# S5 recurrence of a streaming encoder step: one pass over all channel groups, or two passes over half of them

## The reference, cut to what matters

```python
a_bar = jnp.exp(lam * step)
b_bar = ((a_bar - 1.0) / lam)[:, :, None] * b_mat
bu = jnp.einsum('gph,blgh->blgp', b_bar, ug.astype(jnp.complex64))
bu = bu.at[:, 0].add(a_bar[None] * h0)
_, h = lax.associative_scan(_linear_recurrence, (a_seq, bu), axis=1)   # h[l] = a_bar*h[l-1] + bu[l]
y = jnp.einsum('gop,blgp->blgo', c_mat, h).real.reshape(bsz, l, D_SSM)
y = y + d.astype(f32) * uf
z = jax.nn.gelu(y)
out = z * jax.nn.sigmoid(z @ w_glu.astype(f32) + b_glu.astype(f32))
return out.astype(u.dtype), h_last.real, h_last.imag
```

## Time and profile before

| what | value |
|---|---|
| median of 3 runs | 2489.22 us (2488.09 to 2496.07) |
| profiled execution, its own time | 2488.07 us |
| its span | 2486.3 us |
| PE busy | 2303.2 us, 93% of the span |
| DVE, ACT, POOL busy | 44%, 40%, 47% of the span |
| mean granted TensorE clock | 0.969 of full |
| `ssm_run`, first matmul to first instruction of the next stage | 384.53 to 505.67 us |

### The profile page before, as it was taken

One profiled execution on the slowest core, in us unless ns is written; L12 is line 12 of the kernel. 1 busy time (PEld: TensorE's weight loads), 2 busy tenths in 40 slices (PEclk: granted clock), 3 DMA queues, 4 the chain that ended last, 5 costly groups with the idle time before them and its releaser, 6 DMA issues.

```text
span 2486.3 us, 32536 instructions
## 1 busy us (share of the span) xinstructions
PE 2303.2 (93%) x12461; PEld 2107.6 (85%) x12461; DVE 1088.6 (44%) x2093; ACT 1006.8 (40%) x1664; POOL 1167.8 (47%) x557
## 2 busy tenths in 40 slices
PE   6999926789868999999999999999999999999998
PEld 6999914445467999999999999999899999999998
DVE  3786774347654243444253343253343243432222
ACT  4555412147534343443344343344343343343432
POOL 3544575004334555554545454444454444455554
PEclk9999968899888999999999999999999999999999
DMA  5544410114115434355333354433354333344443
GB/s 142 145 132 128 103 41 5 1 50 96 61 51 150 129 116 119 115 152 149 119 101 113 104 164 122 119 102 106 98 156 125 115 102 110 107 132 136 131 127 103
DMA packets 542831, 272.13 MB, mean 109 GB/s; under 512 B 107292, under 2 KB 535893, under 8 KB 542165
## 3 DMA queue, kind: packets, MB, share of 16 engines
q1 hardware_dynamic: 542677, 270.06, 38.2%
HBM read 252.65 MB, written 17.43 MB: 109 GB/s over the span
## 4 chain that ended last, share of the span: by engine, by line
PE 69%; DVE 2%; issue 1%; DMA 0%; ACT 0%; POOL 0%; SPq 0%; DVEq 0%; ACTq 0%
PE ffn_bank L138 22%; PE ffn_bank L139 22%; PE ffn_bank L140 22%; PE ffn_bank L2356 1%; PE ffn_bank L2445 1%; PE ffn_bank L2327 1%; DVE ffn_nv L2060 0%; DVE ffn_mt L2070 0%; ACT ffn_w_hi L1807 0%; POOL ffn_w_lo L1797 0%; DMA ahead_w_raw<-in_w_down 0%; DMA ahead_w_raw<-in_w_gate 0%; DVE ffn_mt L2006 0%; DVE ffn_xm_lo L2107 0%; DVE ffn_xf_lo L2202 0%
## 5 line engine op out<-in xcount | busy, mean ns | idle before, releaser
L1797 POOL TENSOR_TENSOR ffn_w_lo<-ahead_w_raw,ffn_w_hi 128x1024 fp32r<-128x1024 f32 (+1 forms) x380 | 889.2, 2342 | 915.0 <-ACT ffn_w_hi L1807 914.8
L138 PE MATMUL ffn_bank<-ffn_xf_hi,ffn_w_hi 128*128 128x386 f32 (+5 forms) x1760 | 628.7, 357 | 15.4 <-DVE ffn_xf_lo L2202 11.4
L139 PE MATMUL ffn_bank<-ffn_xf_lo,ffn_w_hi 128*128 128x386 f32 (+5 forms) x1760 | 622.8, 354 | 0.0
L140 PE MATMUL ffn_bank<-ffn_xf_hi,ffn_w_lo 128*128 128x386 f32 (+5 forms) x1760 | 621.9, 353 | 0.0
L1807 ACT ACTIVATE ffn_w_hi<-ahead_w_raw 128x1024 fp32r<-128x1024 f32 (+1 forms) x380 | 391.7, 1033 | 505.9 <-PE ffn_bank L140 325.2
L138 PEld LDWEIGHTS ffn_bank<-ffn_xf_hi,ffn_w_hi 128*128 128x128 f32 x1760 | 332.4, 189 | 31.3 <-issue 16.8
L139 PEld LDWEIGHTS ffn_bank<-ffn_xf_lo,ffn_w_hi 128*128 128x128 f32 x1760 | 333.5, 189 | 12.9 <-issue 0.7
L140 PEld LDWEIGHTS ffn_bank<-ffn_xf_hi,ffn_w_lo 128*128 128x128 f32 x1760 | 333.0, 189 | 12.2
L138 PE MATMUL ffn_bank<-ffn_h_hi,ffn_w_hi 128*128 128x384 f32 (+2 forms) x880 | 312.4, 355 | 4.7 <-DVE ffn_xT L2150 3.6
L139 PE MATMUL ffn_bank<-ffn_h_lo,ffn_w_hi 128*128 128x384 f32 (+2 forms) x880 | 310.9, 353 | 0.0
L140 PE MATMUL ffn_bank<-ffn_h_hi,ffn_w_lo 128*128 128x384 f32 (+2 forms) x880 | 309.9, 352 | 0.0
(11 more groups left out here) (342 smaller groups left out, 3075.2 us busy)
## 6 DMA issues: line engine op xcount, KB each, us to landing
ahead_w_raw<-in_w_gate SPq DMA_DIRECT2D x220, 256.0 KB, 3.3
ahead_w_raw<-in_w_up SPq DMA_DIRECT2D x220, 256.0 KB, 3.2
ahead_w_raw<-in_w_down SPq DMA_DIRECT2D x160, 256.0 KB, 3.2
pin_w_raw<-in_w_in SPq DMA_DIRECT2D x120, 256.0 KB, 3.4
ahead_w_raw<-in_w_out SPq DMA_DIRECT2D x160, 128.0 KB, 2.7
ahead_w_raw<-in_w_down SPq DMA_DIRECT2D x80, 192.0 KB, 2.7
pin_xrow<-in_x_prompt SPq DMA_DIRECT2D x15, 512.0 KB, 6.1
out_y_prompt<-ffn_yrow SPq DMA_DIRECT2D x15, 512.0 KB, 4.8
```

Source lines behind the costliest of these rows:

```text
L138: pe.matmul(out, w_hi, x_hi, start=first, stop=False)
L139: pe.matmul(out, w_hi, x_lo, start=False, stop=False)
L140: return pe.matmul(out, w_lo, x_hi, start=False, stop=last)
L1797: pool.tensor_tensor(w_lo[n % 3][:, 0:c], w_raw[n % 2][:, 0:c], w_hi[n % 3][:, 0:c].bitcast(F32), ALU.subtract).then_inc(s_lo, 1)
```

## The change

The table's correction, the rotations, the scans and the edges run twice, each time over four of the eight pairs (`ps`), the first half first. `s_e` and `s_fin` count to 2, DVE starts a half when that half's table and its eight copies of `M` are there, the scratch `T` is half as wide, and the SP writes wait for the second half. On PE the loop is now by half: `direct` of the half's eight outputs in a row, a wait for that half's `s_fin`, `by_state` of the eight in a row.

```diff
-        T = [S["bs"][:, i * PAIRS * CP:(i + 1) * PAIRS * CP].rearrange("p (a c) -> p a c", a=PAIRS) for i in range(2)]
+        HALF = PAIRS // 2
+        T = [S["bs"][:, i * HALF * CP:(i + 1) * HALF * CP].rearrange("p (a c) -> p a c", a=HALF) for i in range(2)]
...
-            sp.wait_ge(s_fin, 1)
+            sp.wait_ge(s_fin, 2)
...
-            t0, t1 = G[0][:, :, 0:CP], G[1][:, :, 0:CP]
-            tt(t0, E[0][:], E[0][:], ALU.mult)
...
-            pool.tensor_tensor(E[1][:], E[1][:], t0, ALU.mult).then_inc(s_e, 1)
+            for half in range(2):
+                ps = slice(half * HALF, (half + 1) * HALF)
+                x, y = E[0][:, ps, :], E[1][:, ps, :]
+                t0, t1 = G[0][:, ps, 0:CP], G[1][:, ps, 0:CP]
+                tt(t0, x, x, ALU.mult)
+                tt(t1, y, y, ALU.mult)
+                tt(t0, t0, t1, ALU.add)
+                chain.link(pool.tensor_scalar(t0, t0, -0.5, 1.5, ALU.mult, ALU.add))
+                tt(x, x, t0, ALU.mult)
+                pool.tensor_tensor(y, y, t0, ALU.mult).then_inc(s_e, 1)
...
-            dve.wait_ge(s_e, 1)
-            dve.wait_ge(s_mev, 4 * 4)
...
+            for half in range(2):
+                ps = slice(half * HALF, (half + 1) * HALF)
+                dve.wait_ge(s_e, half + 1)
+                dve.wait_ge(s_mev, 2 * HALF * (half + 1))
+                rotate(M, ALU.add, ALU.subtract, ps, [(pr, slice(0, CP), plain(ps, pr)), (sm, es, plain(ps, sm))])
+                for i in range(2):
+                    h0 = (h0r, h0i)[i]
+                    for p in range(half * HALF, (half + 1) * HALF):
...
+                rotate(M, ALU.subtract, ALU.add, ps, [(pr, slice(0, CP), shifted(ps, pr, 0)), (sm, es, shifted(ps, sm, 1))])
+                for i in range(2):
+                    dve.memset(G[i][:, ps, 0:1], 0.0)
+                    ins = dve.tensor_copy(G[i][:, ps, CP:CP + 1], (h0r, h0i)[i][:, ps].unsqueeze(2))
+                ins.then_inc(s_fin, 1)
...
-            for n in range(8):
-                direct(n)
-            pe.wait_ge(s_fin, 1)
-            for n in range(2 * L):
-                if n >= 8:
-
-                    pe.wait_ge(s_z, n - 7)
+            for half in range(2):
+                for n in range(half * L, (half + 1) * L):
+                    if half:
+                        pe.wait_ge(s_z, n - L + 1)
                     direct(n)
-                by_state(n)
+                pe.wait_ge(s_fin, half + 1)
+                for n in range(half * L, (half + 1) * L):
+                    by_state(n)
```

More of the change, by code:

```diff
@@ L874, in _, with rotate @@
             chain = Chain(dve, s_chain)
-            dve.wait_ge(s_e, 1)
-            dve.wait_ge(s_mev, 4 * 4)
             pr, sm = slice(0, CP), slice(CP, NC)
             es = slice(0, NC_S)
-            def rotate(o, a, op0, op1, parts):
+            def rotate(a, op0, op1, ps, parts):
                 for (cols, ecols, to) in parts:
@@ L884, in rotate @@
                     t0, t1 = T[0][:, :, 0:n], T[1][:, :, 0:n]
[L885 to L886 removed]
+                    dve.tensor_tensor(t0, a[0][:, ps, cols], E[0][:, ps, ecols], ALU.mult)
+                    chain.link(dve.tensor_tensor(t1, a[1][:, ps, cols], E[1][:, ps, ecols], ALU.mult))
                     to(0, t0, t1, op0)
[L888 removed]
@@ L889, in rotate @@
-                    chain.link(dve.tensor_tensor(t1, a[0][:, :, cols], E[1][:, :, ecols], ALU.mult))
+                    dve.tensor_tensor(t0, a[1][:, ps, cols], E[0][:, ps, ecols], ALU.mult)
+                    chain.link(dve.tensor_tensor(t1, a[0][:, ps, cols], E[1][:, ps, ecols], ALU.mult))
                     to(1, t0, t1, op1)
-            def plain(cols):
-                return lambda i, t0, t1, op: chain.link(dve.tensor_tensor(G[i][:, :, cols], t0, t1, op))
-            rotate(G, M, ALU.add, ALU.subtract, [(pr, slice(0, CP), plain(pr)), (sm, es, plain(sm))])
@@ L896, in _, with plain @@
[L896 to L899, removed]
-                    ins = dve.tensor_tensor_scan(M[i][:, p, sm], rho[:, p:p + 1].to_broadcast([P, NC_S]), G[i][:, p, sm], h0[:, p:p + 1],
-                                                 ALU.mult, ALU.add)
-            chain.link(ins)
-            def shifted(cols, j):
+            def plain(ps, cols):
+                return lambda i, t0, t1, op: chain.link(dve.tensor_tensor(G[i][:, ps, cols], t0, t1, op))
@@ L906, in to, with shifted @@
+            def shifted(ps, cols, j):
                 def to(i, t0, t1, op):
                     n = cols.stop - cols.start
-                    dve.tensor_tensor(G[i][:, :, cols.start + 1:cols.stop], t0[:, :, 0:n - 1], t1[:, :, 0:n - 1], op)
-                    chain.link(dve.tensor_tensor(fin[i][:, j, :], t0[:, :, n - 1], t1[:, :, n - 1], op))
-                return to
-            rotate(G, M, ALU.subtract, ALU.add, [(pr, slice(0, CP), shifted(pr, 0)), (sm, es, shifted(sm, 1))])
-            for i in range(2):
-                dve.memset(G[i][:, :, 0:1], 0.0)
-                ins = dve.tensor_copy(G[i][:, :, CP:CP + 1], (h0r, h0i)[i][:].unsqueeze(2))
```

11 lines of the change are left out of this document (6 added, 5 removed).

## The result

The changed kernel takes 2476.23 us (median of 4 runs, 2475.95 to 2477.77) where the kernel before, in the same rounds, took 2492.64 (4 runs, 2488.09 to 2496.67): a ratio of 0.993 with the interval 0.9914 to 0.9946, so it is faster, by 0.7%. I had forecast 2463, with a range up to 2471. The measured time lies above all of it. The profiled execution took 2477.77, span 2476.0: 10.3 less than the span before, where 25.5 were forecast. What happened is in kind my second rival, the state writes on the path, at 0.13 and 2469 to 2470, and it was larger than I had priced it. That PE and ACT stand during those writes was also one of my signs of being wrong.

The account below looks back on a forecast made before the run. PE needed all four DVE passes before any state part, and DVE all eight pairs before its first. Saving 25.5 us (20.6 waiting, 4.9 alternation and hole) from 2488.07 gave 2462.6, forecast 2463; own range 2459 to 2466, with rivals 2454 to 2471.

Parts of the forecast that it names:

- my second rival: State writes hit the finish: a 6.4 us delay of the last GELU lands on the path, 2469 to 2470; chance 0.13.
- my signs of being wrong: DVE's second half ending after PE's direct parts, PE or ACT standing during state writes, or later stages not following the gate.
- DVE half by half: DVE's rotations, scans and edges: 23.3 us a half; first half 399.8 to 431.6 including 8.5 of hold, second ends 454.9.
- the hold: DVE's first rotation beside POOL's table for the second half: they exclude each other, costing DVE 8.5 us (bounds 0 and 9).
- The row of another stage: Profile rows 6 and 7: DVE's 384-column instruction beside POOL took 2.37 us, the next of that width 0.55.
- PE's wait: PE after tile 0's direct parts, from 426.4: waits 5.2 us for DVE's first half instead of 25.8.
- The eight state parts behind the wait: PE's first state block: 9.1 us, partly at the lower clock, against 7.0 at full clock; ends at 440.7.
- the block of direct parts: PE's direct parts of tile 1 in one row: 16.05 us, as tile 0's, ending at 456.8.
- the second wait for DVE: PE before the second state block: no wait, as DVE's second half ends at 454.9, 1.9 us earlier.
- The gate to the next stage: The next stage starts 15.75 us after the gate, so the gate's shift counts as the shift of the end.
- All rivals but the second: No DVE/POOL hold: 2456, 0.20; hold at every instruction: 2499, 0.02; split brings nothing: 2488 to 2490, 0.03.
- the one on SP: SP's eight state writes, from near 454.9 to near 479.4, stay 0.7 us inside the stage's end at 480.1.

Follow-up runs that it names:

- the kernel with half writes: The changed kernel with single-number state writes issued half by half, eight transfers of 256 numbers after each half's states; 2473.45 us.
- the kernel with runs of eight: The changed kernel with its eight state writes at the same time, each as 64 pieces of 32 bytes instead of 512 of 4; 2462.75 us.

## Why the prediction was wrong

**What held.** DVE half by half was right to 0.3 us at both ends, in part by luck: its first half began 1.95 us later than forecast (401.75), as M was complete later, and the hold was 7.0 us, not 8.5 (14.3 for the first half's rotation, 7.3 for the second's), so that the two errors cancelled. The row of another stage from which I took the hold gave the right kind of answer. PE's wait was 1.75 us shorter than forecast because PE, too, began 2.0 later. The eight state parts behind the wait, partly at the lower clock, took 8.9 us against 9.1, the block of direct parts 16.05, the second wait for DVE nothing. The gate to the next stage is 15.75. All rivals but the second are refuted by their own marks: a hold there was, but for POOL's instructions alone, and the halves cost what halves cost.

**The step that failed** is the one on SP, "costs nothing, or up to 1 or 2 us", with the price of the second rival. I took the writes for costly only if SP were late with them; SP's issue ended at 465.53 and it was never the last, but PE and ACT stood while they ran. I had the rows that speak of it: a packet of instructions of 7.0 us beside the writes, a hole with releaser "issue", an activation after 6.42 us of waiting. I read them as one unlucky packet, argued that this packet would be asked for before the writes, and gave 0.13. That packet was indeed earlier (in 434 to 435 us of the changed kernel, 1.2 us); but the next one, which in the kernels without single numbers comes near 461 and takes 1.0 us, came only at 466.9, while the writes ran, and took 4.3. And it is not about packets of instructions alone: PE, SP and the signals to ACT are all held up, in different kernels in different shares, and in the kernel that signals ACT only once PE resumed before any packet came. The second term that I missed is that the old order had hidden it: there the writes ran beside alternating outputs that cost 2.2 us more for it, and ACT's 6.42 us had slack. The change moved the writes beside the quick state parts and the last GELU, where the same hold costs most in these runs. Priced from the earlier trace rows the rival gave 6.4; it cost 12.7.

**Shown**: single-number state writes cause the loss (rows, or runs of eight at the same moment, remove it), and half as many are enough for most of it. What ACT lacks, by the recorded semaphore events, is PE's signal, not its own instructions. **Open**: what delays the signals, what PE lacks in its holes, and whether the size or the number of the pieces counts. The Trainium skill (Runtime: NRT & Kernel Launch, Instruction fetch mechanics) calls refills mostly hidden; in the kernels without single numbers the packet of 1.0 us left no hole, as it says. With them the packet was slow, but in the kernel with half writes PE resumed at 468.54, before that packet's time was over (463.9 + 6.2), and in the kernel that signals ACT once the hole ended before the packet came, so the packet alone does not explain the holes. The Trainium skill (DMA: Bandwidth & Descriptors, Specifications) says that transfers below 512 bytes are done by read-modify-write; of the two kinds below it here, 4096 pieces of 4 bytes held the engines and 512 of 32 did not, so falling under that size is not by itself enough. The pile-up of pieces, a number that decides, and an overlap in time have each been refuted as the one cause; for PE's holes, signals that it can't send too.

## What to carry to other kernels

A small output written number by number is not free because it is small and off the path: look at which engines stand while it runs, with releasers "issue" and "remote", and ask what will stand beside it after the change. Turn such an output into rows before it is written: here that was worth 12 to 14 us behind the change and 2 without it. When an order of work is judged, ask what each wait will cover, not only what the order itself costs.

## What the runs showed of the hardware

- 2048 writes of 4 bytes, 8 KB in all, were recorded as done within 5 us, and ACT's last GELU still came 12 us after the last of them: the signal from PE was recorded 9.7 us after the matmul that sends it, in the kernel with runs of eight within 0.1.
- A piece of 4 bytes was recorded with 7.3 ns on average at first and with 109 ns later in the same burst, where half still took 9 ns or less and a few took over 1 us. In the kernel with runs of eight all pieces together took 7.8 ns (640 in 5.2% of 454 to 460 us), and none slowed.
- Holding is mutual: beside DVE's rotation POOL's 2.36 us became 3.21, as DVE's 1.22 became 3.3.
